# Attention's compressed branch for four heads at once in the projection's last panels, and the first output panel in the scan

## The reference, cut to what matters

```python
x = x + jnp.concatenate([mix, mem_out], axis=-1) @ w_out[layer]     # first block's output projection
u = rms_norm(x, norm_ffn_g[layer]) @ w_ff1[layer]
...
s_c = jnp.einsum('bqgrd,bngd->bgrqn', qi, kc) * scale - slopes * d_c  # 31 compressed keys, 4 heads r of each group g
p_c = masked_softmax(s_c, d_c >= 0)
o_c = jnp.einsum('bgrqn,bngd->bqgrd', p_c, vc)
...
return gi[..., 0:1] * o_c + gi[..., 1:2] * o_s + gi[..., 2:3] * o_w   # compressed, selected, window
```

## Time and profile before

| | us |
|---|---|
| median of 3 runs (1869.82 to 1874.13) | 1871.87 |
| the profiled execution | 1875.57 |
| its span | 1873.8 |
| PE busy in it | 1802.7 |
| DVE busy in it | 1264.7 |
| ACT busy in it | 944.7 |

### The profile page before, as it was taken

One profiled execution on the slowest core, in us unless ns is written; L12 is line 12 of the kernel. 1 busy time (PEld: TensorE's weight loads), 2 busy tenths in 40 slices (PEclk: granted clock), 3 DMA queues, 4 the chain that ended last, 5 costly groups with the idle time before them and its releaser, 6 DMA issues. The chain is left out here.

```text
span 1873.8 us, 37533 instructions
## 1 busy us (share of the span) xinstructions
PE 1802.7 (96%) x15453; PEld 1568.7 (84%) x15453; DVE 1264.7 (67%) x1977; ACT 944.7 (50%) x1661; POOL 314.1 (17%) x355
## 2 busy tenths in 40 slices
PE   7999988879999999999998899999999999999998
PEld 6777777758988998878976678999999998999997
DVE  4346666556776766567457748777777787777776
ACT  6633444435544444345347747554445675544444
POOL 4012565613300000000023304000003331000000
PEclk9999999999999999999989999999999999999999
DMA  5222000002322333272200031333333222333332
GB/s 190 90 68 69 25 3 4 12 24 72 109 91 90 98 105 113 74 157 83 78 1 1 1 112 58 102 102 102 102 102 113 68 80 68 103 103 104 105 111 74
DMA packets 152239, 148.30 MB, mean 79 GB/s; under 512 B 13677, under 2 KB 150027, under 8 KB 152075
## 3 DMA queue, kind: packets, MB, share of 16 engines
q1 hardware_dynamic: 151948, 145.91, 25.1%
q10 hardware_dynamic: 126, 0.04, 0.0%
HBM read 143.84 MB, written 2.10 MB: 78 GB/s over the span
## 5 line engine op out<-in xcount | busy, mean ns | idle before, releaser
L1725 DVE TENSOR_TENSOR weight_low<-weight_ring,weight_high 128x1024 fp32r<-128x1024 f32 (+2 forms) x250 | 254.0, 1024 | 148.2 <-ACT weight_high L1713 148.2
L1713 ACT CAST weight_high<-weight_ring 128x1024 fp32r<-128x1024 f32 (+2 forms) x250 | 215.2, 865 | 245.9 <-PE psum L247 115.0
L1760 PE MATMUL psum<-tail_x_high,weight_high 128*128 128x256 f32 x1008 | 283.0, 281 | 0.9 <-DVE weight_low L1725 0.6
L1761 PE MATMUL psum<-tail_x_low,weight_high 128*128 128x256 f32 x1008 | 282.5, 280 | 0.0
L1762 PE MATMUL psum<-tail_x_high,weight_low 128*128 128x256 f32 x1008 | 282.5, 280 | 0.0
L1760 PEld LDWEIGHTS psum<-tail_x_high,weight_high 128*128 128x128 f32 x1008 | 189.7, 188 | 3.5 <-DVE weight_low L1725 1.0
L1761 PEld LDWEIGHTS psum<-tail_x_low,weight_high 128*128 128x128 f32 x1008 | 189.8, 188 | 1.6
L1762 PEld LDWEIGHTS psum<-tail_x_high,weight_low 128*128 128x128 f32 x1008 | 189.7, 188 | 0.0
L245 PE MATMUL psum<-tail_hidden_high,weight_high 128*128 128x512 f32 (+1 forms) x480 | 176.6, 368 | 2.5 <-DVE tail_hidden_low L4402 2.5
L246 PE MATMUL psum<-tail_hidden_low,weight_high 128*128 128x512 f32 (+1 forms) x480 | 176.1, 367 | 0.0
L247 PE MATMUL psum<-tail_hidden_high,weight_low 128*128 128x512 f32 (+1 forms) x480 | 176.0, 367 | 0.0
(11 more groups left out here) (531 smaller groups left out, 4572.0 us busy)
## 6 DMA issues: line engine op xcount, KB each, us to landing
weight_ring<-in_w_ff SPq DMA_DIRECT2D x32, 1024.0 KB, 5.3
weight_ring<-in_ffn_w_gate SPq DMA_DIRECT2D x22, 1024.0 KB, 5.5
weight_ring<-in_ffn_w_up SPq DMA_DIRECT2D x22, 1024.0 KB, 5.4
weight_ring<-in_ffn_w_down SPq DMA_DIRECT2D x32, 512.0 KB, 4.7
weight_ring<-in_rw_in SPq DMA_DIRECT2D x11, 1024.0 KB, 5.4
weight_ring<-in_attn_w_in SPq DMA_DIRECT2D x9, 1024.0 KB, 5.2
weight_ring<-in_ffn_w_down SPq DMA_DIRECT2D x8, 768.0 KB, 4.7
weight_ring<-in_w_out SPq DMA_DIRECT2D x4, 1024.0 KB, 4.9
```

Of the source, the lines that this page charges most:

```text
L1713: last = act.copy(high, source)
L1725: last = dve.tensor_tensor(low, source, high, ALU.subtract)
L1760: pe.matmul(out, w_hi, x_hi, start=kk == 0 and not more, stop=False, skip_group_check=more)
L1761: pe.matmul(out, w_hi, x_lo, start=False, stop=False, skip_group_check=more)
```

## The change

In the scan, `MixOperand` moves into `Close`: ACT and DVE split the blocks of `mixed` as they are made, the memory heads first, and PE multiplies them with panel 0 of `w_out` at the scan's end, into banks 4 and 5. SP loads the last panel of `w_out` there too. In the middle, PE begins with panel 1, and DVE adds the first residual blocks at once. Several tiles get other places.

In the attention, the four compressed steps go. A new class `Compressed` handles four heads (a group) at once: scores with the keys as the stationary operand, so that four heads with 32 keys each fill 128 partitions of one bank; ACT copies them, PE transposes them to tokens by keys, DVE, ACT and POOL do the softmax and scaling on 512 columns, PE transposes back and ACT keeps the result. `attn_project` places this in the last three panels. The values of the compressed branch are added in the slc steps by two more matmuls per step, before the others. `TokenSteps` has the remaining 12 steps, with FoX first. Scores are signalled bank by bank, piece 4 is copied by ACT instead of DVE, and the heads are taken out by DVE alone. ACT now does the exponentials of both heads of step s + 1 before the copy of piece 0 of step s. DVE's first lowering waits until PE is through with the projection.

```diff
 class Close:
+        self.k.load_panels(sp, self.k.first_panel["w_out"] + 4)
...
+    def first_output(self, pe):
+        k, mix = self.k, self.mix
+        w_hi, w_lo = k.panel(pe, k.first_panel["w_out"], 0, 0, KT, PW)
+        for blocks in (mix.order[0:6], mix.order[6:KT]):
+            for m in range(2):
+                at = slice(m * P, (m + 1) * P)
+                if blocks[0] == mix.order[0]:
+                    pe.wait_ge(self.scaled, 5 + m)
+                for b in blocks:
+                    mix.ready(pe, b)
+                    last = product(pe, k.ps[:, 4 + m, :], (w_hi[:, b, at], w_lo[:, b, at]), mix.halves(b), b == mix.order[0], b == mix.order[-1])
+        last.then_inc(k.panel_used, 1)
...
     def act(self, act):
+        act.wait_ge(self.read, NCH - 1)
+        for b in self.mix.order[0:2]:
+            self.mix.high_of(act, b)
...
+            if i >= 3:
+                self.mix_high(act, i - 3)
         self.root(act, PAIRS - 1)
+        for i in range(PAIRS - 3, PAIRS):
+            self.mix_high(act, i)
...
         for i in range(PAIRS):
             scale(i)
+            if i == PAIRS - 1:
+                mix_low(i - 3)
             if i:
                 gate(i - 1)
+            if i in (2, 3, 5):
+                mix_low(i - 2)
         gate(PAIRS - 1)
+        for i in range(PAIRS - 2, PAIRS):
+            mix_low(i)
...
+class MixOperand:
+    order = (6, 7, *Close.order)
...
 def attn_project(...):
-            if s == first_of[n_panels - 1]:
+            if s == first_values + 1:
                 for wait in keys_ready:
                     pe.wait_ge(*wait)
-                first_step.scores(pe, 0)
+                cmp.scores(pe, 0)
+                cmp.scores(pe, 1)
+            if s == second_values:
+                cmp.turn(pe, 0)
+                cmp.turn(pe, 1)
+            if s == last_values:
+                cmp.back(pe, 0)
+                pe.wait_ge(cmp.floored, 5)
+                pe.wait_ge(*freed(n_panels - 3))
+                ahead.scores(pe, 0, (0, 1, 2))
+            if s == last_values + 1:
+                cmp.back(pe, 1)
+                pe.wait_ge(*freed(n_panels - 2))
+                ahead.scores(pe, 0, (3, 4))
...
+class Compressed:
+    def scores(self, pe, g):
+        for h in range(self.heads):
+            out = self.bank(g)[32 * h:32 * h + 32]
+            last = pe.matmul(out, a.kc[:, g, :], a.nq[:, self.heads * g + h, :].bitcast(F32), start=True, stop=True)
+        last.then_inc(self.scored, 1)
...
+class TokenSteps:
+    def mix(self, pe, s):
+        if kind == "slc":
+            for e in range(2):
+                v, w = self.cmp.values(2 * i + e)
+                pe.matmul(outs[e], v, w, start=True, stop=False)
...
         @block.vector
+            dve.wait_ge(*projected)
+            self.lower(dve, 0)
+            self.lower(dve, 1)
+            self.weigh(dve, 0)
+            self.weigh(dve, 1)
+            for s in range(self.n):
+                if s + 1 < self.n:
+                    self.lower(dve, 2 * s + 2)
+                    self.lower(dve, 2 * s + 3)
+                    self.weigh(dve, 2 * s + 2)
                 if s:
+                    self.keep(dve, s - 1)
+                self.copy_piece(dve, s, 1)
+                if s + 1 < self.n:
+                    self.weigh(dve, 2 * s + 3)
+                self.copy_piece(dve, s, 3)
...
         @block.scalar
+            for s in range(self.n):
+                if s + 1 < self.n:
+                    self.exps(act, 2 * s + 2)
+                    self.exps(act, 2 * s + 3)
+                self.copy_piece(act, s, 0)
+                if s + 1 < self.n:
+                    self.scale(act, 2 * s + 2)
+                self.copy_piece(act, s, 2)
+                self.copy_piece(act, s, 4)
+                if s + 1 < self.n:
+                    self.scale(act, 2 * s + 3)
```

More of the change, by code:

```diff
@@ L2507, in attn_project @@
     n_low = sum(len(parts_of(s)[1]) for s in parted)
-    keys_ready = [(low, n_low), (kept_gates, 3), (kc_low, 1), (picked, 1), (steep_low, 1)]
+    copies = 2 + P // 32
+    keys_ready = [(low, n_low), (kept_gates, copies), (picked, 1), (steep_low, 1)]
+    cmp, (first_values, second_values, last_values) = ahead.cmp, (first_of[n] for n in range(n_panels - 3, n_panels))
     @block.sync
@@ new lines, in lower, with exps @@
+            dve.tensor_tensor_reduce(self.z[:, at, self.z_at[t]:self.z_at[t] + n], self.k.ps[:, bank, c:c + n], bias, by, 3e38,
+                                     ALU.add, ALU.min, self.top[:, at, t:t + 1]).then_inc(self.lowered, 1)
+    def exps(self, act, u):
+        at = u % self.slots
+        if u >= self.slots:
+            act.wait_ge(self.weighted, u - self.slots + 1)
+        for i, t in enumerate(self.tiles[u % 2]):
+            act.wait_ge(self.lowered, TT * u + i + 1)
+            here = self.z[:, at, self.z_at[t]:self.z_at[t] + (t + 1) * P]
+            last = act.activation(here, here, ACT.Exp, bias=self.top[:, at, t:t + 1],
+                                  scale=-1.0, accum_out=self.total[:, at, t:t + 1])
+        last.then_inc(self.exped, 1)
@@ new lines, in mix @@
+    def mix(self, pe, s):
+        a, (kind, i) = self.a, self.steps[s]
+        for n in (self.n_pieces * (s + 1) - 2, self.n_pieces * (s + 1) - 1):
+            pe.wait_ge(*self.copied(n))
+        if s == 0:
+            pe.wait_ge(self.cmp.kept, GROUPS)
+        elif self.first_of_head(s):
+            pe.wait_ge(self.kept, self.heads_before(s))
+        outs = [self.k.ps[e * HD:(e + 1) * HD, self.out_bank, :] for e in range(2)]
+        if kind == "slc":
+            for e in range(2):
+                v, w = self.cmp.values(2 * i + e)
+                pe.matmul(outs[e], v, w, start=True, stop=False)
+        for j in range(TT):
+            for e in range(2):
+                v = {"fox": a.fv[:, j, (2 * i + e) * HD:(2 * i + e + 1) * HD] if kind == "fox" else None,
+                     "slc": a.vs[:, j, (i // 2) * HD:(i // 2 + 1) * HD], "win": a.vw[:, j, (i // 2) * HD:(i // 2 + 1) * HD]}[kind]
+                last = pe.matmul(outs[e][:, j * P:T], v, self.w_T[:, e, self.w_at[j]:self.w_at[j] + T - j * P],
+                                 start=kind == "fox" and j == 0, stop=kind != "slc" and j == TT - 1)
+        last.then_inc(self.mixed, 1)
@@ L2995, in _ @@
         @block.vector
         def _(dve):
-            def add(s):
-                if steps[s][0] == "win":
-                    block = heads[:, block_of(s), :]
-                    dve.wait_ge(mixed, s + 1)
-                    dve.wait_ge(kept, steps[s][1] + 1)
-                    dve.tensor_tensor(block, ps[:, out_bank, :], block, ALU.add).then_inc(kept, 1)
-            for s in range(n_steps):
-                ahead = (2 * s + 2, 2 * s + 3) if s + 1 < n_steps else ()
-                for u in ahead:
-                    lower(dve, u)
-                if s:
-                    add(s - 1)
-                for n in pieces_of(s):
-                    if pieces[n][2] == "dve":
-                        copy_piece(dve, n)
-                for u in ahead:
-                    weigh(dve, u)
@@ new lines, in _ @@
+            self.exps(act, 1)
+            self.scale(act, 0)
+            self.scale(act, 1)
+            for s in range(self.n):
+                if s + 1 < self.n:
[8 more added lines that the diff above has]
+                    self.scale(act, 2 * s + 3)
```

646 lines of the change are left out of this document (309 added, 337 removed).

## The result

| | before | after |
|---|---|---|
| median, us | 1872.10 (4 runs, 1869.82 to 1874.13) | 1850.26 (4 runs, 1849.73 to 1851.10) |
| profiled execution, us | 1875.57 | 1851.10 |
| its span, us | 1873.8 | 1849.4 |
| PE / DVE / ACT busy, us | 1802.7 / 1264.7 / 944.7 | 1783.1 / 1253.6 / 948.9 |

The change makes the kernel faster: the ratio of after to before is 0.9884, 95% interval 0.9867 to 0.9901. The forecast was 1851.0, 0.7 us above the median; the range was 1843 to 1861. The spans differ by 24.4 us where 20.9 were forecast.

What follows compares the result with a forecast made beforehand. PE was taken as the bound, busy 1802.7 of 1873.8 us. Gains of 7.4 and 13.5 us sum to 20.9: span 1852.9, profiled time 1854.7, median 1851.0, range 1843 to 1861.

Steps and rivals of the forecast that it cites:

- Part A: Scan's end: first output panel moved into the scan, so panel 1 starts at 417.1 instead of 424.49, gaining 7.4 us.
- Projection: Attention's projection from the first value panel, with compressed scores, transposes and FoX scores added, ends at 948.1 without a gap.
- X: Time when PE is through with attention's projection and the token steps' pipeline starts empty, forecast at 948.
- The choice of 2.2 instead of 6.9: Projection's compressed scores: 2.2 us if a group's four column tiles run side by side, 6.9 if each matmul runs alone.
- Fill: Start of attention's steps, pipeline empty: first value sum ends at X + 20.1 plus 3.3 us for the clock, 971.4.
- the 3.3: Charge in attention's first step for one 6.6 us stretch at clock 0.50, half lost: 3.3 us.
- Steps: Eleven attention steps after the first: 8.45 us each, slc 9.05, the one with FoX's scores 9.35; 93.2 us together.
- part B: Attention: four compressed steps replaced by work in the projection and slc steps; end at 1064.6 against 1078.1, gaining 13.5 us.
- tiles don't overlap: Rival in attention: added value matmuls and compressed scores run one after another, 7.5 us more, 1858.5 us; chance 0.12.
- part A yields nothing: Rival at the scan's end: moved casts push the last root, the boundary costs PE 5 us; 1858.4 us, chance 0.08.
- The smoother start: Rival at attention's first step: clock stays 1.00, ACT's queue is better; 3.3 and 1.5 us return, 1846; chance 0.14.
- The slower rival: Attention's steps: copy 0 behind both exponentials brings low clock to eleven steps, 3.3 us each, 36 us, 1887; chance 0.04.

Runs made afterwards that it cites:

- the experiment: Changed kernel with all four heads' compressed scores of a group written through one column tile instead of four: 1855.31 us, ratio 0.9902.
- the kernel with transposes: Changed kernel plus 36 unused identity transposes on PE in step 0's waits (8 before the first piece, 28 before the third): 1847.82 us, ratio 0.9867.
- the other execution of the change: The changed kernel run again unaltered, as the mark beside the follow-up runs: 1850.93 us, ratio 0.9883.
- the padding run: Changed kernel with 128 bytes of unused memory ahead of the middle block's and attention's tiles: 1849.42 us; with 256 bytes, 1849.54 us.

## Why the prediction was right

**Part A.** The forecast put panel 1 at 417.1 and it stands at 417.30; the casts hid, PE's largest idle time was 0.33 us and the clock stayed at 1.00. The step that was off is how far one trace stands for all: in the 7.4 us stood 2.8 for the low clock behind the gap, and the kernel with part A undone lost about 1.5 there. On medians part A is worth 6.1.

**Projection.** 43.1 us were forecast from the first value panel to X, 42.0 measured (896.01 to 938.05). The two score groups took 1.86 and not 2.2, the 16 transposes 1.5 (0.8 behind 909.58, 0.4 behind 921.84 and behind 930.23) and not 2.2, and the waits of 0.2 and 0.15 are not to be seen; the panels took 34.7 where 34.6 was laid out, and the FoX scores their 3.9. The choice of 2.2 instead of 6.9 is what the forecast hung on here, and the experiment confirms the row it was read from.

**Fill.** A wait of 4.65 us ahead of the third piece was laid out from the order on ScalarE, and it is there with 4.46. X + 20.1 plus 3.3 for the clock were forecast, X + 22.2 came. Without the clock's share it is 20.1, the sum that was laid out: the pieces behind the wait took 2.6 us where the kernel with transposes needs 1.8, and the scores 5.3 instead of 4.0, 2.1 us in all. The mis-sized term is the 3.3, taken as half of a stretch of 6.6 us. The windows put some 7 us at the lower level, but 1.3 of them fell on the wait, where there was nothing to slow down, and the other 5.5 cost 2.1, less than half. It is also no fixed number: the other execution of the change lost 1.5.

**Steps.** 93.2 us for the eleven later steps were forecast and 93.65 measured (960.23 to 1053.88). A slc and win pair takes 17.7 where 17.5 was laid out, and the step with FoX's scores 9.46 where it was 9.35. No step brought the low clock back.

**What the forecast did not have.** 1.7 us of faster matmuls in the middle, 1.4 of them in the feed-forward layer. That stretch moved with the tiles' places in the padding run and stayed when part A was undone. Which tile matters, and why, is open.

**The rule that was weighed.** The Trainium skill, TensorEngine Tiling (Array Packing), Restrictions and Gotchas, has it that different row tiles can't access one PSUM bank at the same time. The slc steps' pair of heads lies on row tiles 32 apart and writes one bank, and it takes 1.07 us, as the old pair on one row tile did. One after the other they would take 1.7, two times 0.86. The trace disagrees with the rule as the forecast read it. The two write different partitions of the bank (0 to 63 and 64 to 127), as the small matmuls of the scan did; no run here has two row tiles on the same partitions of one bank, so for that case nothing is shown.

**The sum.** Part A came to 7.2 in the traces (7.4 forecast), part B to 15.4 (13.5), the middle to 1.7 (0), together 24.3 of span. The median fell by only 21.8, where 20.9 were forecast: the profiled execution of the kernel before lay 3.5 us above its median, that of the change 0.8. Of these 2.7 us the longer low clock behind the old gap may be 1.3 (14.1 against 12.8 for panel 0); that isn't shown, since only one execution of the kernel before has a trace. Where the rest lies is open. So part of the closeness is luck. The forecast took its gain from one long execution as if the median would fall by as much, and the unforeseen 1.7 and the 1.9 of part B made up for it.

**The rivals.** That tiles don't overlap is excluded by the kernel on one column tile; that part A yields nothing, by the one with part A undone. The smoother start did not happen by itself, but it could be made: reordering step 0 gave 1846.4. That is the very size that the rival named, by luck in its parts: it gave the clock 3.3 and the queue 1.5, and in the traces it was 2.1 and 2.9, less 0.7 in the steps behind. The slower rival is a true mechanism that this change avoids. The kernel with the copy between the exponentials has a wait of 2.1 us in ten steps, the clock falls to 0.87 over them and the time is 1880.5 where 1887 was worked out. Spread over eleven steps the 29.6 us are 2.7 a step, where the forecast had 3.3 and let the rival decide from 1.9. The forecast erred only in the cause that it named: copy 0 behind both exponentials is what protects the steps. It also read too much out of the gaps alone. Those around 970 in the kernel before, which it gave as a reason for this rival, were 0.53 and 0.37 us; the change has 0.64 and 0.33 in every other step and keeps 1.00. What else in the old compressed steps brought the low clock, with their 16 small matmuls and a softmax between, no run tells.

## What to carry to other kernels

An order of work on a helper engine is right for the full pipeline or for the filling one, seldom for both: write the first step out by itself before changing the loop. When a loop closes over two engines, ask for each small copy what it waits for before asking what waits for it; a copy that must wait for TensorE has to stand behind the work that doesn't. Cost a wait of TensorE twice, once as idle time and once by the clock behind it, and charge the second only for matmuls that really run in it. And look at the busy time when a gain is explained: here the idle time from the first value panel to the end of the attention hardly changed.

## What the runs showed of the hardware

- Four fp32 matmuls of 512 columns on four column tiles of 32 take 0.93 us together (two groups in 1.86), against 3.5 on one column tile (6.98 for two groups).
- Idle transposes held the granted clock: 0.54 became 1.00 in one place, where they filled 3.2 us of a 4.5 us wait, and 0.87 became 0.97 over the steps; the medians fell by 3.1 and 12.9 us.
- The same gap is not always followed by the same low clock: 5.15 us by some 3 us at 1.2 GHz in one execution and some 6 in another, 4.46 us by a loss of 2.1 and 1.5 us in two executions of one kernel, and near the start 3.56 us by none where 3.30 was followed by a mean of 0.72 over 12 to 24 us.
- A VectorE subtraction between SBUF tiles of 128x512 took 0.68 us with POOL nearly idle. Started inside an add of POOL of the same size it ended 0.54 to 0.55 us after the add, up to 1.76 us in all; products with both inputs in SBUF that began just ahead of an add kept 0.68 and 0.69, and the add took 1.66 and 1.79 instead of 1.27.
- The same gapless matmuls of the feed-forward layer took 287.0, 285.6, 284.8 and 285.6 us with tiles in four placements, the last three 128 bytes apart (one trace each of the first and the last).
